# Attention values with the stationary side swapped to two column halves, softmax ahead of convolution taps, and GpSimd's taps in a sum of their own

## The chip, the cores and the metric
The kernel is one program on one core of a Trainium2 chip. The metric is the device time of one execution in microseconds (us); lower is better. A core has TensorE (PE, matmuls; PEld is its weight load), VectorE (DVE), ScalarE (ACT), GpSimd (POOL) and SyncE (SP, which here issues most transfers). They run side by side and wait for each other by semaphores. Matmul results land in PSUM, which holds eight banks of 512 f32 per partition; everything else is in SBUF.

## The reference
256 positions of 1024 channels go through two stacks of two layers each.

```
# stack 1, per layer: rmsnorm -> w_in (14 groups of 256 columns) -> four branches -> w_out, added to x
y_a = conformer_conv(a_u, a_v, ...) * silu(a_z)      # 31-tap depthwise convolution, layernorm, silu
y_b = short_gated_conv(b_b, b_c, b_x, w) * silu(b_z)
y_c = window_gqa(c_q, c_k, c_v, sink) * silu(c_z)    # 4 heads of 64, rope, softmax with a sink logit
y_d = neighborhood_attn(d_q, d_k, d_v, rpb) * silu(d_z)   # 4 heads of 64, learned bias
x = x + concat(y_a, y_b, y_c, y_d) @ w_out
# stack 2, per layer: swiglu FFN, mixer (forgetting attention, dilated attention, HGRN2 recurrence), swiglu FFN
x = x + 0.5 * swiglu(rmsnorm(x), wg, wu, wd)
x = x + concat(fox_attention, dilated_attention, hgrn2) @ w_out
x = x + 0.5 * swiglu(rmsnorm(x), wg, wu, wd)
```

Each attention is softmax(q k^T + bias) v for 256 queries and 256 keys in 4 heads. For the change only this counts: out[query, h] = sum over keys of p[query, key] * v[key, h] / (sum over keys of p), and in stack 1 the result times the gate silu(z).

## The kernel before
**Slots.** The work is a sequence of weight slots. A slot is 128x2048 f32: one group of 256 columns of w_in, two row blocks of w_out, or a part of an FFN matrix. SP loads it into `w_raw`, ACT rounds it (`round_hi`, line 455, w_hi), DVE subtracts (`split_lo`, line 872, w_lo), and PE multiplies hi*hi, hi*lo and lo*hi (lines 1593 to 1595; 1633 and 1636 in the FFN). Three slots are in flight (RING = 3): the load of slot i waits for the split of slot i-3, and the rounding of slot i+3 waits until PE is done with slot i.

**Order.** All order is written out by hand, each engine has one queue, and the queues meet by semaphores. In a mixer, "step i" is projection i of 14 (`ORDER_1`: a_u, a_v, c_q, c_kv, d_q, d_k, d_v, c_z, d_z, b_c, b_x, b_b, b_z, a_z); then four slots of w_out follow. After projection i PE does small work between the big projections.

**Attention units.** A mixer has four units u of 128 queries and 4 heads (two units for each of two attentions), spread over steps 7 to 13, with step i = 7 + u as the start of unit u:
- step 7+u: PE `scores` (line 1733; each head's 64 channels lie on one half of the partitions), DVE `soft` (bias add and row maximum, lines 947 to 956), ACT `softmax_exp` (line 515)
- step 8+u: PE `turn_probs` (transposes, line 1744), ACT `pt_copy` of the transposed probabilities to pT (line 565), DVE `finish` (1/sum)
- step 9+u: PE `values` (line 1753: pT is stationary, 128x128; v moves, 64 columns; result is queries x channels in `mix`), ACT `normed_output` (line 542: four scaled copies `mix` to `o_tm`)
- step 10+u: PE turns o_tm back to channels x queries in `aux` (lines 1823, 1967, 1997), DVE gates it in stack 1 (`gated_y`, line 1104) and splits it to y_hi and y_lo (lines 879, 880); in stack 2 `plain_y` only splits.

In stack 2 the two units with u even have only 128 keys (`causal_keys`), so half the matmuls and transposes. Each f32 matmul shows as two instructions in the profile, each transpose as one. Within a step PE's order is values, turn_probs, scores, output turn.

**DVE's order in a step of stack 1.** Copy of the projection out of PSUM (line 937), then 2 or 3 convolution taps (`taps`, line 1090) in steps 2 to 9, then `finish` and `soft`, then `split_lo` of slot i+3, then gates; in steps 4 and 5 the rope rotation (`rotate`, lines 982 to 987) comes last, and `gated_y` comes last too.

**Convolution.** 31 taps on two channel halves c. DVE sums taps 0 to 19 of half 0. ACT multiplies the other 42 (`tap_products`, line 532) but one into a ring of 5 buffers `fz`, POOL adds them (`add_product`, line 1496): the 31 taps of half 1 first, then, after waiting for DVE's last tap (`conv_part`), the last 11 of half 0 into DVE's sum. `conv_ready` lets PE turn the result (`conv_to_tm`) in the first w_out slot; layernorm statistics follow on DVE (line 1123), POOL takes the root (line 1454), DVE applies it (line 1143), and PE turns it back (line 1840) in the second w_out slot.

**Norms.** POOL's `norm` makes 1/rms by a power (lines 1453, 1454; for the double norm between the stacks lines 1537, 1538), and PE's `spread_rows` (line 1665) spreads it over columns. At the end of a section DVE (`section_end`) adds to x, splits h and splits the first slots of the next section.

Of the kernel before, what the change touches and what calls it, by code (L numbers as in the profile page):

```python
# [23 lines left out]
NH = 4  # L24
# [26 lines left out]
for _i, _n in enumerate(["hq0", "hq1", "hf0", "hf1", "hi0", "hi1", "hg0", "hg1"]):  # L51
# [11 lines left out]
DVE_TAPS = 20  # L63
# [14 lines left out]
                  if kind in ("left", "right") or (kind == "turn" and i in (7, 8)) or (kind == "out" and i >= 10)]  # L78
               + ["cross", "ho0", "out13", "ho1", "hn0", "hn1"])
# [73 lines left out]
def stacks_kernel(nc, a, out):  # L153

    with ExitStack() as ctx:
# [22 lines left out]
        o_tm = sb("o_tm", [P, 2, NH * HD])  # L178
# [258 lines left out]
        def _(act):  # L437
# [96 lines left out]
            def normed_output(un, u, turned):  # L534

                c = 4 * (u % 2)
                act.wait_ge(inv_ready, un + u + 1)
                act.wait_ge(mix_written, un + u + 2)
                if u >= 2:
                    act.wait_ge(aux_written, turned)  # L540
                for s_, h in enumerate(HORDER):
                    ins = nc.scalar.activation(o_tm[:, u % 2, h * HD:(h + 1) * HD], mix[:, h * HD:(h + 1) * HD], ACT.Copy,
                                               scale=row_inv[:, c + s_:c + s_ + 1])
                ins.then_inc(mix_read, 1)
# [82 lines left out]
            for l in range(DEPTH):  # L627
                base, base3, un = l * LAYER_1, l * (LAYER_1 // RING), l * 4
                gates = 0
                for i, name in enumerate(ORDER_1):  # L630
# [9 lines left out]
                    if SC_1 + 2 <= i < SC_1 + 6:  # L640
                        normed_output(un, i - SC_1 - 2, l * AUX_1 + i - SC_1)
# [66 lines left out]
            for l in range(DEPTH):  # L708
# [87 lines left out]
                for i, name in enumerate(ORDER_2):  # L796
# [28 lines left out]
                    if SC_2 + 2 <= i < SC_2 + 6:  # L825
                        u = i - SC_2 - 2
                        normed_output(un, u, ax + AUX_IX_2[f"out{i - 1}"] + 1 if u >= 2 else 0)
# [25 lines left out]
        def _(dve):  # L853
# [56 lines left out]
            def section_end(section, base, slots, factor, split):  # L910
# [13 lines left out]
                split_h(n, (2, 3))  # L924
                split_lo(base + slots, 2)
# [40 lines left out]

            def normed_output(un, u):

                c = 4 * (u % 2)
                dve.wait_ge(mix_written, un + u + 2)  # L970
                for s_, h in enumerate(HORDER):
                    ins = v.tensor_scalar(o_tm[:, u % 2, h * HD:(h + 1) * HD], mix[:, h * HD:(h + 1) * HD],
                                          row_inv[:, c + s_:c + s_ + 1], None, ALU.mult)
                ins.then_inc(mix_read, 1)
# [96 lines left out]
            for l in range(DEPTH):  # L1071
# [25 lines left out]
                def gated_y(u, kt):  # L1097
# [4 lines left out]
                    yv = y_f[:, 0:2 * P].rearrange("p (c s) -> p c s", s=P)  # L1102
                    dve.wait_ge(aux_written, n + 1)
                    v.scalar_tensor_tensor(out=yv, in0=aux[:, 0:2 * P].rearrange("p (c s) -> p c s", s=P), scalar=0.5,
                                           in1=g[:, :, cols], op0=ALU.mult, op1=ALU.mult).then_inc(aux_read, 1)
                    dve.wait_ge(aux_read, n + 2)
                    split_y(yv, kt, cols, yc_ready if u < 2 else yd_ready, l * 2 + u % 2 + 1)

                lnx = proj[:, ix["a_v"], :].rearrange("p (t c) -> p t c", t=NT)
                for i, name in enumerate(ORDER_1):  # L1110
                    if i == 0:
                        dve.wait_ge(rb_ready, l + 1)
                    if name != "d_v":
                        copy_out(base, i, name, l * NPROJ + i)
                    if i == 7:
                        step_aux()
                    if i == 13:
                        gated_y(3, 6)

# [19 lines left out]
                    split_lo(base, i + RING)  # L1139
                    if i == 13:  # L1140
# [4 lines left out]
                        ins.then_inc(aux_read, 1)  # L1145
                    if name in ("a_v", "c_z", "d_z", "b_z", "a_z"):
# [14 lines left out]
                    if l == 0 and i == 6:  # L1161
# [10 lines left out]
                    if i == 5:  # L1172
                        rotate(step_aux(), proj[:, ix["c_kv"], 0:S], cst[:, C_COS:C_COS + S],
                               cst[:, C_SIN:C_SIN + S], 1, kc[:, 0, :])
# [875 lines left out]
```

## Time and profile before
| | us |
|---|---|
| median of 3 executions | 1315.42 (1314.92 to 1316.31) |
| the profiled execution | 1318.41 |
| its span, first to last instruction | 1316.5 |
| first stack | up to about 280 |
| FFNs and mixers of the second stack | from there to the end |

The profile is of one execution. Start times are us from the start of the span. "Busy" of PE contains the modelled end of each matmul, so a matmul shows some 270 ns while another starts every 110 ns: what a matmul costs PE is the distance between starts, which the chain of waits gives (the length of a piece divided by its number of instructions). The granted clock is a share of 2.4 GHz: 1.00 is 2.4 GHz and 0.50 is 1.2 GHz.

### The profile page before, as it was taken

The numbers are of one execution on the slowest core, as the hardware profiler recorded it, in microseconds if no ns is written. First come the engines' busy times: TensorE is split into PE (matmuls) and PEld (weight loads), VectorE is DVE, ScalarE is ACT, GpSimd is POOL, SyncE is SP. The second block draws the span as 40 slices with busy tenths as digits, with TensorE's granted clock in tenths as the row PEclk, the third lists the DMA queues.
The fourth block names the chain that finished last, engine by engine and source line by source line (L and its number), as shares of the span: only waits on it lengthen the run. The fifth ranks groups of instructions, "written<-read, shape, count | busy, mean of one in ns | idle before, by whom it ended". The sixth has DMA issues, their size and how long they took to land.

```text
span 1316.5 us, 21360 instructions
## 1 busy us (share of the span) xinstructions
PE 1288.8 (98%) x8100; PEld 1155.2 (88%) x8100; DVE 978.0 (74%) x1172; ACT 699.1 (53%) x957; POOL 276.0 (21%) x261
## 2 busy tenths in 40 slices
PE   7999999999999999999999999999999999999997
PEld 7989998988888899998888888888889998888886
DVE  5787787779777769767877778877776967777776
ACT  5575457564444487645444445444458663644443
POOL 3655165447000023201000007300011410100000
PEclk9999999999999999999999999999999999999999
DMA  9745473357666545335666665766654524666661
GB/s 275 238 129 152 163 218 122 118 161 206 195 188 189 181 133 184 101 97 160 206 188 189 188 187 162 216 188 189 193 157 142 160 97 127 189 202 188 188 192 50
DMA packets 271551, 224.03 MB, mean 170 GB/s; under 512 B 16012, under 2 KB 254358, under 8 KB 271478
## 3 DMA queue, kind: packets, MB, share of 16 engines
q1 hardware_dynamic: 268720, 217.61, 54.8%
q0 software_dynamic: 880, 2.11, 0.9%
q10 hardware_dynamic: 1878, 3.32, 0.7%
q8 instruction: 48, 0.79, 0.2%
q14 instruction: 25, 0.20, 0.0%
HBM read 221.83 MB, written 3.14 MB: 171 GB/s over the span
## 4 chain that ended last, share of the span: by engine, by line
PE 85%; DVE 7%; ACT 3%; DMA 2%; issue 2%; POOL 1%; SPq 0%; DVEq 0%; POOLq 0%; ACTq 0%
PE wide L1633 24%; PE wide L1636 13%; PE big L1593 8%; PE big L1594 8%; PE big L1595 8%; PE wide L1593 5%; PE wide L1594 5%; PE wide L1595 5%; DVE w_lo L872 2%; DMA w_raw<-in_w_in 2%; PE wide L1902 2%; PE wide L1753 2%; PE big L1733 1%; PE big L1744 1%; ACT w_hi L455 1%
## 5 line engine op out<-in xcount | busy, mean ns | idle before, releaser
L872 DVE TENSOR_TENSOR w_lo<-w_raw,w_hi 128x2048 fp32r<-128x2048 f32 x203 | 471.8, 2325 | 103.0 <-ACT w_hi L455 102.3
L455 ACT ACTIVATE w_hi<-w_raw 128x2048 fp32r<-128x2048 f32 x204 | 389.8, 1912 | 195.3 <-PE big L1595 129.2
L1633 PE MATMUL wide<-h_both,w_hi 128*128 128x512 f32 x1408 | 356.7, 393 | 0.0
L1633 PEld LDWEIGHTS wide<-h_both,w_hi 128*128 128x128 f32 x1408 | 254.6, 189 | 48.6 <-DVE h_both L895 2.0
L1593 PE MATMUL wide<-h_both,w_hi 128*128 128x256 f32 x720 | 208.8, 290 | 0.0
L1636 PEld LDWEIGHTS wide<-h_both,w_lo 128*128 128x128 f32 x1408 | 194.2, 190 | 15.0
L1594 PE MATMUL wide<-h_both,w_hi 128*128 128x256 f32 x720 | 204.1, 284 | 0.0
L1595 PE MATMUL wide<-h_both,w_lo 128*128 128x256 f32 x720 | 204.0, 283 | 0.0
L1636 PE MATMUL wide<-h_both,w_lo 128*128 128x256 f32 x1408 | 198.8, 282 | 0.0
L1593 PE MATMUL big<-w_hi,y_hi 128*128 128x512 f32 x480 | 189.4, 395 | 0.0
L1594 PE MATMUL big<-w_lo,y_hi 128*128 128x512 f32 x480 | 187.3, 390 | 0.0
L1595 PE MATMUL big<-w_hi,y_lo 128*128 128x512 f32 x480 | 187.0, 390 | 0.0
L678 ACT ACTIVATE work<-wide 128x512 f32<-128x512 f32 x88 | 52.5, 597 | 235.3 <-PE wide L1636 235.3
L1453 POOL TENSOR_SCALAR small<-small 128x1 f32<-128x1 f32 (+1 forms) x22 | 4.8, 216 | 796.4 <-ACT probs L459 733.9
L1593 PEld LDWEIGHTS wide<-h_both,w_hi 128*128 128x128 f32 x720 | 138.6, 193 | 3.5 <-issue 2.6
L1594 PEld LDWEIGHTS wide<-h_both,w_hi 128*128 128x128 f32 x720 | 138.7, 193 | 0.1
L1595 PEld LDWEIGHTS wide<-h_both,w_lo 128*128 128x128 f32 x720 | 138.4, 192 | 0.0
L1207 DVE TENSOR_TENSOR work<-wide,work 128x512 f32<-128x512 f32 x88 | 60.7, 690 | 88.1 <-ACT work L678 88.1
L1595 PEld LDWEIGHTS big<-w_hi,y_lo 128*128 128x128 f32 x480 | 90.1, 188 | 19.3
L1593 PEld LDWEIGHTS big<-w_hi,y_hi 128*128 128x128 f32 x480 | 90.3, 188 | 16.9
L1594 PEld LDWEIGHTS big<-w_lo,y_hi 128*128 128x128 f32 x480 | 90.4, 188 | 16.5
L1496 POOL TENSOR_TENSOR work<-work,fz 128x256 f32<-128x256 f32 x82 | 89.9, 1097 | 53.9 <-ACT fz L532 37.1
(247 smaller groups left out, 1536.2 us busy)
## 6 DMA issues: line engine op xcount, KB each, us to landing
w_raw<-in_w_in SPq DMA_DIRECT2D x112, 512.0 KB, 4.7
w_raw<-in_ffn_w_gate SPq DMA_DIRECT2D x88, 512.0 KB, 4.0
w_raw<-in_ffn_w_up SPq DMA_DIRECT2D x88, 512.0 KB, 5.2
w_raw<-in_ffn_w_down SPq DMA_DIRECT2D x88, 512.0 KB, 4.1
w_raw<-in_w_out SPq DMA_DIRECT2D x32, 512.0 KB, 4.3
work<-rpb_shifted SPq DMA_DIRECT2D x32, 64.0 KB, 4.1
rpb_shifted<-rpb_rows POOLq DMA_DIRECT2D x2, 735.0 KB, 8.2
pT<-in_gains ACTq DMA_DIRECT2D x2, 512.0 KB, 5.3
```

The source lines that it names most:

```text
L455: nc.scalar.activation(w_hi[:, r, :], w_raw[:, r, :], ACT.Copy).then_inc(hi_ready, 1)
L678: nc.scalar.activation(tmp_cross[parity].rearrange("p (c s) -> p c s", s=S), wide[:, 2 * parity:2 * parity + 2, S:2 * S], ACT.Copy).then_i ...
L872: v.tensor_tensor(w_lo[:, r, :], w_raw[:, r, :], w_hi[:, r, :].bitcast(F32), ALU.subtract).then_inc(lo_ready, 1)
L1207: v.tensor_tensor(both, wide[:, 2 * parity:2 * parity + 2, 0:S], tmp_cross[parity].rearrange(view, s=S), ALU.add).then_inc(pj_read[parity], 1)
L1496: g.tensor_tensor(acc, acc, fz[:, n % PROD_RING, :], ALU.add).then_inc(prod_used, 1)
L1593: t_.matmul(o, a_hi, b_hi, start=first, stop=False, skip_group_check=True)
L1594: t_.matmul(o, a_hi, b_lo, start=False, stop=False, skip_group_check=True)
L1595: return t_.matmul(o, a_lo, b_hi, start=False, stop=last, skip_group_check=True)
L1633: t_.matmul(o, hi[:, kt, c], h_both[:, kt].rearrange("p a s -> p (a s)"), start=kt == 0, stop=False, skip_group_check=True)
L1636: ins = t_.matmul(o[:, 0:S], lo[:, kt, c], h_hi[:, kt, :], start=False, stop=kt == KT - 1, skip_group_check=True)
L1753: ins = t_.matmul(mix[:, h * HD:(h + 1) * HD], pT[:, (2 * s_ + kt) * P:(2 * s_ + kt + 1) * P], v_of(h, kt), start=kt == 0, stop=kt == keys ...
L1902: ins = t_.matmul(aux[:, h * P:(h + 1) * P], key[:, h * S + tk * P:h * S + (tk + 1) * P], query[:, h * S + tq * P:h * S + (tq + 1) * P], s ...
```

## The change
- `values`: v (128x64) is stationary, the transposed probabilities move (128 columns). Heads 2c and 2c+1 write partitions 0 to 63 and 64 to 127 of the same 128 columns of `mix`. The result is already channels x queries, so `o_tm`, ACT's `normed_output` and the output turn go.
- The scale 1/sum now is needed along the columns: PE spreads it (`spread_inverse`), again in two column halves, into `aux`. In stack 1 DVE multiplies it with the gate and then with `mix`; in stack 2 ACT copies it to SBUF (`inverse_copy`) and DVE multiplies.
- Outputs come one step earlier (u - 2 instead of u - 3). PE does scores ahead of turn_probs.
- Stack 1, DVE: rotations right after the copy; softmax, then gated_y, then taps, then the split. The split of slot 9 moves from step 6 to behind softmax in step 7. Taps are dealt 3, 3, 2, 2, 3, 0, 2, 2, 2, 1 over steps 2 to 11.
- POOL sums its 11 taps of half 0 into a separate buffer and adds that to DVE's sum at the end, so it no longer waits in the middle.
- Between the stacks DVE waits for both roots before it splits slot 2.
- The copies of the sink logits move from step 6 to step 2.

```diff
-DVE_TAPS = 20
+DVE_TAPS_AT = {2: 3, 3: 3, 4: 2, 5: 2, 6: 3, 8: 2, 9: 2, 10: 2, 11: 1}
+DVE_TAPS = sum(DVE_TAPS_AT.values())
...
-        o_tm = sb("o_tm", [P, 2, NH * HD])
+        inv_rows = sb("inv_rows", [P, 2, 2 * P])
...
-            def normed_output(un, u, turned):
...
+            def inverse_copy(u, written):
+                act.wait_ge(aux_written, written)
+                nc.scalar.activation(inv_rows[:, u % 2, :], aux[:, 0:2 * P], ACT.Copy).then_inc(aux_read, 1)
...
                 split_h(n, (2, 3))
+                if n == DEPTH:
+                    dve.wait_ge(rstd_ready, rms_count(n) * 2 + 2)
                 split_lo(base + slots, 2)
...
                 def gated_y(u, kt):
+                    scaled_gate = tmp[:, 0:2 * P].rearrange("p (c s) -> p c s", s=P)
                     dve.wait_ge(aux_written, n + 1)
-                    v.scalar_tensor_tensor(out=yv, in0=aux[:, 0:2 * P]..., scalar=0.5,
+                    v.scalar_tensor_tensor(out=scaled_gate, in0=aux[:, 0:2 * P]..., scalar=0.5,
                                            in1=g[:, :, cols], op0=ALU.mult, op1=ALU.mult).then_inc(aux_read, 1)
                     dve.wait_ge(aux_read, n + 2)
+                    dve.wait_ge(mix_written, un + u + 2)
+                    v.tensor_tensor(yv, mix[:, 0:2 * P]..., scaled_gate, ALU.mult).then_inc(mix_read, 1)
+                    dve.wait_ge(mix_read, un + u + 2)
                     split_y(yv, kt, cols, ...)
...
+                    if i == 4:
+                        rotate(step_aux(), proj[:, ix["c_q"], :], ...)
+                    if i == 5:
+                        rotate(step_aux(), proj[:, ix["c_kv"], 0:S], ...)
...
-                        gated_y(3, 6)
...
-                    if 2 <= i < 10:
-                        taps((i - 2) * DVE_TAPS // 8, (i - 1) * DVE_TAPS // 8)
-                    if i == 9:
-                        dve.sem_inc(conv_part, 1)
...
-                    split_lo(base, i + RING)
+                    if 0 <= u - 2 < 4:
+                        gated_y(u - 2, 4 if u - 2 < 2 else 6)
+                    if i == 7:
+                        split_lo(base, 6 + RING)
+                    if i in DVE_TAPS_AT:
+                        done = sum(n for at, n in DVE_TAPS_AT.items() if at < i)
+                        taps(done, done + DVE_TAPS_AT[i])
+                        if done + DVE_TAPS_AT[i] == DVE_TAPS:
+                            dve.sem_inc(conv_part, 1)
...
+                    if i != 6:
+                        split_lo(base, i + RING)
...
                 def plain_y(i, kt):
-                    aux_in(f"out{i}")
+                    aux_freed(f"out{i}")
+                    dve.wait_ge(mix_written, un + u + 2)
+                    v.tensor_tensor(yv, mix[:, 0:2 * P]..., inv_rows[:, u % 2, :]..., ALU.mult).then_inc(mix_read, 1)
                     split_y(yv, kt, cols, ...)
...
+                part = inv_rows[:, 0, :]
+                link(g.memset(part, 0.0))
                 for k, (c, j) in enumerate(POOL_TAPS):
-                    if (c, j) == (0, DVE_TAPS):
-                        pool.wait_ge(conv_part, l + 1)
...
-                    add_product(l * PRODS + k - 1, conv_acc[:, c])
-                pool.sem_inc(conv_ready, 1)
+                    add_product(l * PRODS + k - 1, conv_acc[:, c] if c else part)
+                pool.wait_ge(conv_part, l + 1)
+                g.tensor_tensor(conv_acc[:, 0], conv_acc[:, 0], part, ALU.add).then_inc(conv_ready, 1)
...
             def values(n, v_of, keys=S):
-                for s_, h in enumerate(HORDER):
+                for c in range(2):
                     for kt in range(keys // P):
-                        ins = t_.matmul(mix[:, h * HD:(h + 1) * HD], pT[:, (2 * s_ + kt) * P:(2 * s_ + kt + 1) * P],
-                                        v_of(h, kt), ...)
+                        for low in range(2):
+                            at = (2 * HORDER[2 * c + low] + kt) * P
+                            ins = t_.matmul(mix[low * HD:(low + 1) * HD, c * P:(c + 1) * P], v_of(2 * c + low, kt),
+                                            pT[:, at:at + P], ...)
+            def spread_inverse(n, u):
+                pe.wait_ge(inv_ready, n + 1)
+                for c in range(2):
+                    for low in range(2):
+                        at = 4 * (u % 2) + HORDER[2 * c + low]
+                        ins = t_.matmul(aux[low * HD:(low + 1) * HD, c * P:(c + 1) * P],
+                                        row_inv[:, at:at + 1].to_broadcast([P, HD]), ident, start=True, stop=True, ...)
...
-                    if 0 <= u - 1 < 4:
-                        turn_probs(l * 4 + u - 1, u - 1)
                     if 0 <= u < 4:
...
+                    if 0 <= u - 1 < 4:
+                        turn_probs(l * 4 + u - 1, u - 1)
-                    if 0 <= u - 3 < 4:
+                    if 0 <= u - 2 < 4:
                         aux_free()
-                        pe.wait_ge(mix_read, l * 4 + u - 3 + 2)
-                        for c in range(2):
-                            ins = t_.transpose(aux[:, c * P:(c + 1) * P], o_tm[...], ident)
-                        ins.then_inc(aux_written, 1)
+                        spread_inverse(l * 4 + u - 2, u - 2)
```

## Rows read from the trace of the kernel before

**Rows 1.** Page, busy us (share of the span) and instructions of two engines.
```profile
PE 1288.8 (98%) x8100; PEld 1155.2 (88%) x8100; DVE 978.0 (74%) x1172; ACT 699.1 (53%) x957; POOL 276.0 (21%) x261
```

**Rows 2.** Waits of PE: waiting line, what it waited for, us, times, longest.
```profile
PE big L1744 <- ACT small L518: 3.5, 2, 1.8
PE wide L1794 <- DVE tmp L982: 2.5, 1, 2.5
PE wide L1840 <- DVE proj L1143: 1.3, 2, 0.6
PE big L1665 <- POOL small L1538: 1.1, 1, 1.1
PE wide L1902 <- DVEq L1278: 0.6, 2, 0.3
```

**Rows 3.** Windows, stretch: us, busy (instructions) by engine, PEclk, DMA share, GB/s.
```profile
55.04:58.45 3.41, 3.41 (x16) 3.23 (x16) 3.30 (x6) 1.72 (x4) 3.17 (x4) 0.50 0.95 284
58.45:61.86 3.41, 3.41 (x30) 3.41 (x30) 3.38 (x2) 0.16 (x1) 3.25 (x3) 1.00 0.46 108
208.64:212.05 3.41, 3.41 (x16) 2.26 (x15) 2.72 (x8) 3.30 (x5) 0.00 (x0) 0.50 0.62 186
```

**Rows 4.** Timeline of DVE, layer 0, steps 4 and 5: start, us, what.
```profile
50.05 1.35 DVE L1090 SCALAR_TENSOR_TENSOR work<-work,parA_all 128x256 f32<-128x256 f32 x2
51.43 2.71 DVE L872 TENSOR_TENSOR w_lo<-w_raw,w_hi 128x2048 fp32r<-128x2048 f32 x1
54.07 0.68 DVE L982 TENSOR_TENSOR tmp<-wide,cst 128x512 f32<-128x512 f32 x1
```

**Rows 5.** Timeline of DVE, layer 0, step 7.
```profile
69.69 2.42 DVE L1090 SCALAR_TENSOR_TENSOR work<-work,parA_all 128x256 f32<-128x256 f32 x3
72.14 1.22 DVE L947 SCALAR_TENSOR_TENSOR probs<-big,cst 128x1024 f32<-128x1024 f32 x1
75.35 2.84 DVE L872 TENSOR_TENSOR w_lo<-w_raw,w_hi 128x2048 fp32r<-128x2048 f32 x1
```

**Rows 6.** Timeline of POOL, layer 0, the first 17 products.
```profile
41.48 22.86 POOL L1496 TENSOR_TENSOR work<-work,fz 128x256 f32<-128x256 f32 x17 [8.55 <-ACT fz L532]
```

**Rows 7.** Timeline of DVE, layer 0, step 13.
```profile
123.75 0.41 DVE L1104 SCALAR_TENSOR_TENSOR y_f<-wide,proj 128x256 f32<-128x256 f32 x1
125.52 0.43 DVE L1123 BATCH_NORM_STATS2 bn_raw<-wide 128x6 f32<-128x256 f32 x1
```

**Rows 8.** Timeline of DVE and POOL between the stacks.
```profile
285.66 2.28 DVE L872 TENSOR_TENSOR w_lo<-w_raw,w_hi 128x2048 fp32r<-128x2048 f32 x1
285.74 2.62 POOL L1538 TENSOR_TENSOR small<-small,minus_half 128x1 f32<-128x1 f32 x1
288.70 0.55 POOL L1538 TENSOR_TENSOR small<-small,minus_half 128x1 f32<-128x1 f32 x1
```

**Rows 9.** Chain of waits, layer 0, steps 8 and 9: start, us, what.
```profile
89.96 1.06 PE big L1733 x8
91.02 0.32 PE wide L1593
91.34 0.11 PE wide L1594
96.95 1.73 PE wide L1753 x16
```

**Rows 10.** Chain of waits, second stack, step 7 (L1733 here has 128 columns).
```profile
521.90 0.67 PE wide L1902 x6
522.58 0.65 PE big L1733 x8
```

**Rows 11.** Groups with shapes: line engine op, tiles, shapes xcount | busy us, mean ns | idle before.
```profile
L1753 PE MATMUL wide<-proj,pT 128*128 128x64 f32 x224 | 26.8, 271 | 0.0
L542 ACT ACTIVATE o_tm<-wide,small 128x64 f32<-128x64 f32 x64 | 14.7, 315 | 0.5 <-issue 0.4
L1104 DVE SCALAR_TENSOR_TENSOR y_f<-wide,proj 128x256 f32<-128x256 f32 x8 | 3.3, 417 | 0.1
```

More of the change, by code:

```diff
@@ L77 @@
                + [f"{kind}{i}" for i in range(6, 13) for kind in ("left", "right", "turn", "out")
-                  if kind in ("left", "right") or (kind == "turn" and i in (7, 8)) or (kind == "out" and i >= 10)]
-               + ["cross", "ho0", "out13", "ho1", "hn0", "hn1"])
+                  if kind in ("left", "right") or (kind == "turn" and i in (7, 8)) or (kind == "out" and i >= 9)]
+               + ["cross", "ho0", "ho1", "hn0", "hn1"])
 AUX_2 = len(AUX_ORDER_2)
@@ L825, in _ @@
                     if SC_2 + 2 <= i < SC_2 + 6:
-                        u = i - SC_2 - 2
-                        normed_output(un, u, ax + AUX_IX_2[f"out{i - 1}"] + 1 if u >= 2 else 0)
+                        inverse_copy(i - SC_2 - 2, ax + AUX_IX_2[f"out{i}"] + 1)
                     if SC_2 + 1 <= i < SC_2 + 5:
@@ L1160, in _ @@
                         bounds_shift()
-                    if l == 0 and i == 6:
+                    if l == 0 and i == 2:
+                        dve.wait_ge(table_in, TABLES)
                         for k in range(DEPTH):
@@ L1165, in _ @@
                                               ).then_inc(sink_ready, 1)
+                    if l == 0 and i == 6:
                         dve.wait_ge(const_in, CONSTS)
                         dve.wait_ge(sink_ready, DEPTH * NH)
-                    if i == 4:
-                        dve.wait_ge(table_in, TABLES)
-                        rotate(step_aux(), proj[:, ix["c_q"], :], cst[:, C_COS:C_COS + S], cst[:, C_SIN:C_SIN + S],
-                               2, proj[:, ix["c_q"], :])
-                    if i == 5:
-                        rotate(step_aux(), proj[:, ix["c_kv"], 0:S], cst[:, C_COS:C_COS + S],
-                               cst[:, C_SIN:C_SIN + S], 1, kc[:, 0, :])
-                    if 0 <= u - 3 < 3:
-                        gated_y(u - 3, 4 if u - 3 < 2 else 6)
                 dve.wait_ge(short_conv, l + 1)
@@ L1385, in _ @@
                         rotate(ax2 + AUX_IX_2[f"turn{i}"], q, cos2[:], sin2[:], 2, q)
-                    if 0 <= u - 3 < 3:
-                        plain_y(i, 0 if u - 3 < 2 else 2)
+                    if 0 <= u - 2 < 4:
+                        plain_y(i, 0 if u - 2 < 2 else 2)
                     if name == "hg0":
@@ L1414, in _ @@
                 head_sums(0)
-                plain_y(NPROJ - 1, 2)
                 output_gate(3, NPROJ - 1)
@@ L1954, in _ @@
                                    causal_keys(u))
+                    if 0 <= u - 1 < 4:
+                        turn_probs(l * 4 + 8 + u - 1, u - 1, causal_keys(u - 1))
                     if i in (7, 8):
@@ L1962, in _ @@
                         ins.then_inc(aux_written, 1)
-                    if 0 <= u - 3 < 3:
+                    if 0 <= u - 2 < 4:
                         aux_free(f"out{i}")
-                        pe.wait_ge(mix_read, l * 4 + 8 + u - 3 + 2)
-                        for c in range(2):
-                            ins = t_.transpose(aux[:, c * P:(c + 1) * P], o_tm[:, (u - 3) % 2, c * P:(c + 1) * P], ident)
-                        ins.then_inc(aux_written, 1)
+                        spread_inverse(l * 4 + 8 + u - 2, u - 2)
                 def hgrn_out(t):
@@ L1990, in w_out @@
                     tm_sum(mb, NPROJ + j, j == 0, j == NWOUT - 1, 2 * grp, between)
-                def last_turn():
-                    aux_free(f"out{NPROJ - 1}")
-                    pe.wait_ge(mix_read, l * 4 + 8 + 3 + 2)
-                    for c in range(2):
-                        ins = t_.transpose(aux[:, c * P:(c + 1) * P], o_tm[:, 1, c * P:(c + 1) * P], ident)
-                    ins.then_inc(aux_written, 1)
                 def turn_out(t):
@@ L2008, in _ @@
                 hgrn_out(0)
-                w_out(0, {1: last_turn, 3: lambda: hgrn_out(1)})
+                w_out(0, {3: lambda: hgrn_out(1)})
                 w_out(1, {1: lambda: turn_out(0), 3: lambda: turn_out(1)})
```

48 lines of the change are left out of this document (20 added, 28 removed).

## The prediction, made before the changed kernel was run

> **What bounds the kernel now.** I read the page first: PE is busy 98% of the span, DVE 74%, ACT 53%, POOL 21% [rows 1]. So time can come from two places only: fewer or shorter matmuls, and PE's own waits with what they do to its clock. The view of waits, for PE alone, gives the second: beside the start-up it waits 3.5 us in two waits of the probability transposes for ACT's exponential, 2.5 us once for DVE's rope product, 1.3 us in two waits for the layernorm result, 1.1 us for POOL's root between the stacks, and 0.6 us in two waits of DVE's queue in stack 2 [rows 2]. The windows show what follows: three stretches of 3.41 us, after the rope wait and after each of the two exponential waits (the middle one, at 78.94, is like its neighbours), have a granted clock of 0.50, that is 1.2 GHz, and hold 16 matmuls where the next 3.41 us at 1.00 hold 30 [rows 3]. No wait of PE under 1.7 us is followed by such a stretch. Matmul prices come from the chain of waits.
>
> **Part 1: DVE's order in stack 1.** The rope wait: in step 4 of layer 0 DVE did two taps (1.35) and a split (2.71) ahead of the rotation's first product at 54.07, whose end PE awaited [rows 4]. The rotation now follows the copy and starts at about 50.1, 4.0 us earlier. PE waited 2.5. All of it goes. What moves back is the split of slot 7, by the rotation's 2.3 us to about 56.4; PE needs it after projection 6, at about 58.4.
>
> The exponential waits: in step 7 three taps (2.42) stand ahead of the softmax, which starts at 72.14 [rows 5], and PE waits 1.7 and 1.8 us in the two layers. Now the softmax starts when the scores are there, some 2.4 us sooner; scores go ahead of the transposes, which makes the transposes due 1.1 us later (a scores piece lasts 1.06) [rows 9]. 3.5 us against 1.8 at most: both waits go. Behind the softmax stand two splits of 2.3 each (slots 9 and 10). I laid DVE's queue out step by step for layer 0: split 9 ends at 71.8 and PE wants it at 74.2; split 10 ends at 74.1 and is wanted at 84; the load of slot 12, which waits for split 9, is issued at 72 and rounded at 80. The taps and the gates behind them end by 83, and the copy of projection 9, ready at 80, is late by 3 us but wanted only at 90. So DVE runs late by up to 3 us in steps 8 to 10 without PE seeing it, and is level again in step 11. In steps 9 to 12 it has one more product of 128x256 per unit, of 0.42 like the present one [rows 11], 1.7 per mixer, all in the cover of 5.8 us projections. If that cover were gone each would cost itself, 6.7 in all.
>
> So the waits give 2.5 + 3.5 = 6.0. Without a wait of that length there is no half-clock stretch: each held 16 matmuls in 3.41 us, which at the rate of the next stretch (30 in 3.41, 0.114 each) take 1.8 to 1.9, so 1.5 is lost in each, 4.5 in three [rows 3].
>
> One new wait speaks against this in layer 0. POOL is behind there: its first 17 products last from 41.48 to 64.34, 1.34 each [rows 6]. ACT's step 6 products wait for POOL's ring of five, and behind them in ACT's queue stand the copy of the second key, for which the first scores wait, and in step 7 the first exponential. PE now comes to the scores at 64.3 instead of 68.7; ACT gets its fifth product off at about 64.8 and the copy done at 65.2. I take +0.9 (bounds: 0 if POOL runs at its 1.1 average, +2.5 if the exponential is late too). Below the length of wait that a half clock followed.
>
> **Part 2: POOL's taps.** POOL no longer stops in the middle for DVE's last tap, but waits at the end; DVE's last tap now comes in step 11, at about 104 in layer 0. The final addition, the table transfers of 4.5 us and the short convolution's product follow on POOL's queue, until about 111, when ACT wants them. PE turns the convolution only in the first w_out slot, at about 116. Hidden. With gated_y(3) moved out of step 13, the layernorm statistics no longer wait for its 1.77 us (123.75 to 125.52) [rows 7] but only for PE's transposes, about 0.5 us earlier; PE's wait of 0.64 shrinks by that in both layers: -1.0.
>
> **Part 3: the wait between the stacks.** POOL's power took 2.62 while DVE's split of slot 2 ran from 285.66, and 0.55 once it was over [rows 8]. With DVE holding the split back, both powers are done at about 287.1, PE comes at 288.2 and its 1.1 us goes. The split ends at 289.4; slot 2 is wanted at 292. -1.1. In stack 2 the output turn of step 10 stood behind DVE's plain_y; now ACT frees the bank, and DVE's two queue waits (0.6) go: -0.6. ACT's exponentials of the recurrence come 2 us later in a step, but DVE wants them one step later.
>
> **Part 4: PE's own work.** Before, values are 224 instructions, in the chain 16 in 1.73, so 0.108 each: 24.2 us [rows 9, 11]. They are bound by loading 128 columns, not by the 64 that move. After, there are as many, with 64 stationary and 128 moving columns, in two column halves. How they go no row shows. The nearest is the scores, where heads lie in two row halves: 8 instructions with 256 columns take 1.06, with 128 columns 0.65 [rows 9, 10]. The difference, 0.41, is 4 times 0.103, the passage of 128 more columns for four pairs, not for eight single ones; and a single full-size instruction of 128 columns takes 0.112 (6 in 0.67) [rows 10]. So the two halves run at the same time, and a pair of N = 128 costs about 0.11. I take that for column halves: 112 pairs, 12.3 us, -11.9. Bounds: no overlap, 0.112 each, 25.1, +0.9; overlap and nothing else, -12.5.
>
> `spread_inverse` adds 16 times 8 instructions, 64 pairs of 0.11, 7.0; the 32 transposes that go cost 0.11 each, 3.5. Net +3.5 (without overlap, +10.8).
>
> Changing between full array and halves is not free: the fixed part of the scores is 0.65 - 4 x 0.103 = 0.24, and the first projection matmul behind them takes 0.32 where the next takes 0.11 [rows 9, 10]. So about 0.2 per change, both ways. Before, a mixer of stack 1 has 8 changes (scores in steps 7 to 10). After, steps 9 and 10 go full, columns, rows, full, columns, full (5), step 11 has 4, step 12 has 2: 20. That is 12 more, in stack 2 as well, 48 in four mixers: 9.6 us. In 28 of them the load that stands exposed has half the columns, half of 0.108 less: -1.5. I take +8.1 (bounds: 0, if a change to column halves costs nothing, and 9.6). On this the Trainium skill has a rule, TensorEngine Tiling (Array Packing), Key Properties: changing the tiling mode drains the engine. The 0.2 above agrees for row halves; no row shows it for columns. PE part: -11.9 + 3.5 + 8.1 = -0.3. The swap of the operands is worth nothing by itself; it pays by mode changes for what it saves.
>
> ACT loses 64 copies of 0.23 (14.7 in all) [rows 11] and gets 8 of 0.5; it is off the path.
>
> **The sum.** -6.0 - 4.5 + 0.9 - 1.0 - 1.1 - 0.6 - 0.3 = -12.6. The profiled execution took 1318.4, so 1305.8 on its terms. It lies 3.0 above the median of the three runs shown, 1315.42, so the forecast for the median is 1302.8.
>
> **The rivals.**
> (a) The stall moves. The first exponential, behind ACT's products and POOL's ring, is late again and the clock falls once or twice more. For: POOL's rate in rows 6, and DVE without reserve in steps 7 to 9. Against: by my layout the transposes are due 0.4 us after the exponential. It gives back one or two waits of 1.7 with their 1.5: 1306 to 1309.
> (b) Mode changes cost less than in rows 9 and 10 where one side is a column half: up to -8.1, so 1294.7. For: a row change does not have to be like a column change. Against: the row pieces show it in both directions.
> (c) Column halves do not overlap. Then values keep 25.1 (+12.8 against the forecast), `spread_inverse` costs 14.3 instead of 7.0 (+7.3), and the mode changes stay: 1302.8 + 20.1 = 1322.9, slower than before. The place is all 16 units. The change is slower once more than 13 of these 20 us come true, at two thirds of the overlap lost. For it: both halves read all 128 partitions of the moving side, which row halves don't. Against: nothing in a row.
> (d) The load of a pair is not hidden behind the pair before it. Half of 0.108 for each of 176 pairs, +9.5: 1312.3. In the rows of values, loads run under the matmul before: 0.108 per instruction is the one load, with the 64 moving columns beside it [rows 9, 11]. The Trainium skill says, in TensorE: Matmul & The Clock Gate, Part 3 (Packing small matmuls, The mechanism), that a weight load overlaps matmuls in flight only when they use other rows of the array; two column halves use the same rows. By that rule this rival holds, and the trace of full-size values speaks against the rule.
>
> **How the numbers follow.** Forecast 0.57, (a) 0.14, (b) 0.11, (c) 0.09, (d) 0.09. The predicted time is 1302.8. The forecast's own spread is some 4 us either way (the switch price of 48 changes at 0.03, and the waits). The range takes in (a), (b) and the lower half of (d), and leaves out (c): 1294.5 to 1312. What can be told from no change is 0.2%, 2.6 us. Slower by that needs (c), or (d) with (a): 0.10. Within it, the upper end of (d) or a partial (c): 0.05. Faster: 0.85.
>
> **What would show it.** PE waits for L1744 and L1794 gone from the view of waits, and windows at 1.00 all through stack 1 (else part 1 is wrong). The chain piece of values at about 0.9 + 0.2 for 16 instructions; 1.8 to 2.0 would be (c), 1.3 to 1.5 (d). The first instruction behind a column piece at 0.3 (if 0.1, (b)). A wait of PE's scores for ACT's second key, near 1 us, in layer 0 only. The FFN stretches of stack 2 keep their length. If stack 1 gains under 9 us or the mixers of stack 2 change by more than 3 us each, my sum was wrong even where the total agrees.

## The result, and the profile after

| | before | after |
|---|---|---|
| median of 4 executions, us | 1315.36 (1314.92 to 1316.31) | 1306.22 (1305.99 to 1307.26) |
| profiled execution, its span | 1318.41, 1316.5 | 1306.36, 1304.5 |
| mean granted clock | 0.994 | 0.999 |

The ratio is 0.9931 (95% interval 0.9914 to 0.9948): the changed kernel is 9.1 us faster. The forecast was 1302.8, which is 3.4 us below what came. By the spans of their profiled executions the two kernels lie 12.0 us apart, where the sum had 12.6.

The page after, for [rows 1]. PE and its loads do 6 and 12 us less, with 96 instructions more:
```profile
PE 1282.4 (98%) x8196; PEld 1143.1 (88%) x8196; DVE 989.9 (76%) x1188; ACT 688.4 (53%) x901; POOL 277.1 (21%) x265
```
The waits of PE, for [rows 2] (line, what it waited for, us, times, longest):
```profile
PE big L1740 <- ACT small L519: 2.5, 2, 1.9
PE wide L1907 <- DVE work L1282: 2.4, 4, 0.6
PE wide L1751 <- DVE y_f L1093: 0.4, 2, 0.2
PE wide L1845 <- DVE proj L1140: 0.4, 1, 0.4
PE big L1589 <- DVE y_lo L871: 0.3, 1, 0.3
```
The rope wait, the wait between the stacks and DVE's queue waits are gone. The transposes of the probabilities (L1740, before L1744) still wait for an exponential, but for another: in both layers it is now that of the second unit, 1.9 and 0.6 us. The windows, for [rows 3], and the stretch at the new wait:
```profile
55.04:58.45 3.41, 3.41 (x31) 1.00 0.26 54
208.64:212.05 3.41, 2.80 (x32) 1.00 0.00 0
79.00:82.41 3.41, 2.44 (x28) 1.00 0.72 251
```
The clock stays at 1.00 (2.4 GHz), even around the wait of 1.9.

The reason for the new wait shows in DVE's timeline in steps 7 and 8 of layer 0 (start, us, what; for [rows 5]; some lines left out):
```profile
66.73 1.21 DVE L940 SCALAR_TENSOR_TENSOR probs<-big,cst 128x1024 f32<-128x1024 f32 x1
...
69.72 5.58 DVE L863 TENSOR_TENSOR w_lo<-w_raw,w_hi 128x2048 fp32r<-128x2048 f32 x2
75.23 1.22 DVE L1155 SCALAR_TENSOR_TENSOR proj<-tanh,proj 128x512 f32<-128x512 f32 x1
76.48 0.69 DVE L930 TENSOR_TENSOR proj<-wide,row_scale 128x512 f32<-128x512 f32 x1
...
77.67 1.23 DVE L940 SCALAR_TENSOR_TENSOR probs<-big,cst 128x1024 f32<-128x1024 f32 x1 [0.22 <-DVE small L957]
```
The first softmax comes 5.4 us earlier than before. Behind it stand two splits, 5.58 us with POOL adding beside them (the sum had 2 x 2.3), and a gate; the second softmax starts at 77.67, its exponential at 81.08, and lasts to 83.2.

PE's own pieces are as long as forecast. The first fence is the chain of waits of before, second stack, step 10, the next that of after:
```profile
553.25 1.73 PE wide L1753 x16
554.99 0.45 PE big L1744 x4
555.43 1.09 PE big L1733 x8
```
```profile
542.19 1.02 PE wide L1751 x16
543.22 1.06 PE big L1729 x8
544.28 0.59 PE big L1740 x4
544.87 0.59 PE wide L1760 x8
545.46 0.32 PE wide L1589
```
Sixteen matmuls of values, eight pairs, take 1.02 instead of 1.73. The transposes cost 0.14 more behind a row piece, and `spread_inverse` costs 0.59.

Where the 12.0 us came from, stage by stage. Each number is a difference of the two profiled executions in the distance between the last matmuls of successive slots:

| stage | forecast | came |
|---|---|---|
| rope wait with its half clock | -4.0 | -4.3 |
| first exponential, two layers, with half clock | -6.5 | -7.2 |
| wait for the second key | +0.9 | 0 |
| wait for the second exponential (step 9) | 0 | +2.6 |
| PE's part in the other steps of stack 1 | -0.3 in all | -0.8 |
| layernorm | -1.0 | -1.2 |
| end of layer 0 (w_out waits for `y_lo`) | 0 | +0.8 |
| between the stacks | -1.1 | -1.4 |
| mixers of stack 2, both | -0.6 | -0.4 |
| start | 0 | -0.1 |
| sum | -12.6 | -12.0 |

Parts 1 to 3 were not run one by one. What each is worth is read from the stage in which it acts. In the row of the first exponential, DVE's earlier softmax and PE's scores ahead of the transposes are not told apart.

### The profile page after: what moved, and what is told of

It is laid out like the page before. It is cut to its first block, busy times and chain, and to the rows that moved or that the text cites. A ratio compares the mean times of both kernels' runs of the same rounds, so it can differ in the third digit from the quotient of the medians.

```text
span 1304.5 us, 21499 instructions
## 1 busy us (share of the span) xinstructions
PE 1282.4 (98%) x8196; PEld 1143.1 (88%) x8196; DVE 989.9 (76%) x1188; ACT 688.4 (53%) x901; POOL 277.1 (21%) x265
## 4 chain that ended last, share of the span: by engine, by line
PE 81%; DVE 11%; issue 2%; ACT 2%; DMA 2%; POOL 1%; SPq 0%; DVEq 0%; POOLq 0%; ACTq 0%
PE wide L1629 25%; PE wide L1632 13%; PE big L1589 8%; PE big L1590 8%; PE big L1591 8%; PE wide L1589 4%; DVE w_lo L863 4%; PE wide L1590 4%; PE wide L1591 4%; DMA w_raw<-in_w_in 2%; PE wide L1907 2%; DVE work L1074 1%; PE big L1653 1%; ACT w_hi L456 1%; PE wide L1751 1%
## 5 line engine op out<-in xcount | busy, mean ns | idle before, releaser
L1491 POOL TENSOR_TENSOR work<-work,fz 128x256 f32<-128x256 f32 x60 | 69.2, 1154 | 28.8 <-ACT fz L533 24.9
```

The source lines that it names most:

```text
L1491: g.tensor_tensor(acc, acc, fz[:, n % PROD_RING, :], ALU.add).then_inc(prod_used, 1)
```

## The experiments

Every run was compared with the kernel before on its own chip, whose median lay between 1315.4 and 1316.2; distances to before are the safer figure.

Spans of single executions need a caution. The last matmul of projection 4 in layer 0 starts between 44.6 and 46.0 us (split9_in_6 and split10_in_8), though these two kernels and after (45.2) do the same up to there. Spans "past the start", below, are counted from this matmul to the last projection matmul.

**The kernel before again**, without an edit.

> The kernel before, unchanged, against itself. The profiled execution of before took 1318.41 us, 3.0 above the median of its plain runs; that of after took 1306.36, 0.1 above its own. Theory: nothing is added by profiling; the executions of before differ among themselves in how many of their long PE waits are followed by a stretch of half clock (1.5 us each). Then executions lie between 1314.9 and 1318.5, the longer ones with the lower mean clock, and a profiled one near 1315 shows one or two stretches of 0.50 instead of three. Rival: a profiled execution of before always has its three stretches and takes 1318, and the plain ones differ by something else. Ratio 1.000 by both.

1316.21 us; over the 55 executions of before in the experiments 1313.5 to 1319.1, the shortest with a mean clock of 0.998, the longest with 0.994. The longer ones have the lower clock: on average 1314.6 at a mean clock of 0.998 (7 executions), 1315.5 at 0.997 (23), 1316.4 at 0.996 (21), 1317.7 at 0.995 (2) and 1318.5 at 0.994 (2). Two of the waits of PE in the profile of before_again, and two windows (at the first exponential of layer 0 and of layer 1):
```profile
PE big L1744 <- ACT small L518: 4.6, 2, 2.8
PE wide L1794 <- DVE tmp L982: 1.4, 1, 1.4
```
```profile
75.23:82.06 6.83, 6.14 (x26) 0.50 0.47 154
207.00:210.41 3.41, 2.69 (x21) 1.00 0.25 67
```
The same kernel has here two half-clock stretches' worth instead of three [rows 3]: none after a rope wait of 1.4, a double one at a wait of 2.8, none at the wait of 1.8 in layer 1 that had one before. And the stall moves even without an edit: against the profile of before, step 5 is 2.7 us shorter, step 8 is 2.3 longer, and step 8 of layer 1 is 1.6 shorter. The execution that I had profiled was long by one stretch too many, so most of the 3.0 above the median lay inside the terms that I then removed. The theory holds.

**Parts 1 to 3 alone.** `values`, ACT's scaled copies and the output turns as before, the rest as after (POOL's partial sum in another free buffer).

> Parts 1 to 3 without part 4: DVE's order in stack 1, POOL's taps summed apart, scores ahead of the transposes, the wait between the stacks; values, their scaled copies on ACT and the output transposes stay as before. Theory: this is the whole gain. Rope wait -4.4 and first exponential wait -3.5 per layer less 2 and 0.7 of the new wait for the second exponential, between the stacks -1.4: the profiled execution comes to 1307 to 1309, the median 7 to 9 us under before, ratio 0.993 to 0.995. Rival: the column halves carry a good part of the gain (their matmuls save 11.9 us of PE's time, and only 3.5 + 8.1 of it was argued to be given back); then this kernel stands 3 us or more above after, 1309.5 or more by the median.

1304.95 us, ratio 0.9917 (0.9903 to 0.9930), span 1303.1. This is the whole gain and more: 11.1 us under before, where I had expected 7 to 9 and where after is 9.1 under. Past the start it is 1.1 us shorter than after. Its one wait for an exponential:
```profile
PE big L1753 <- ACT small L519: 1.4, 1, 1.4
```
The exponential of the second unit comes as late as in after, but PE comes later, since its full-size values take 0.7 us longer (1.73 against 1.02): what the column halves save in step 9 turned into waiting, 2.5 us in after's two layers against 1.4 here. In stack 2, where nothing waits for it, after's part 4 costs 0.3 us per mixer against this kernel. The layernorm wait is gone here too, in both layers, though `gated_y(3)` stands where it stood; see below.

**Part 4 alone**, in before's order of DVE and of PE's pieces.

> Part 4 alone: values stationary in two column halves, spread_inverse, the gates on mix and on the spread inverse; DVE's order, the taps, POOL and the order of PE's pieces (transposes ahead of scores) stay as before. Theory: PE's own work comes out even (by the terms of the prediction -11.9 + 3.5 + 8.1), so this kernel is within 2 us of before: 1313.5 to 1316.5, its stack 2 mixers changed by under 0.5 us each, the rope wait and the waits for the exponentials still there. Rival: the column halves gain by themselves, 1311 or less.

1313.78 us, 2.2 under before, ratio 0.9985 (0.9976 to 0.9994). By span it is 1.4 under before_again, past the start 1.9. Of this 0.2 per mixer is in stack 2, as the theory has it. In each layer of stack 1 0.4 is in the second w_out slot, by `gated_y(3)`, and 0.5 in step 12 and the first w_out slot, where turns of outputs are gone. The rope wait is 0.2 longer, which is within what before varies by.

**The halves apart.**
```
-                for c in range(2):
-                    for kt in range(keys // P):
-                        for low in range(2):
+                for low in range(2):
+                    for c in range(2):
+                        for kt in range(keys // P):
```


> After, with the matmuls of values in another order: all of the lower column half first, then all of the upper one, so that neighbours no longer lie in different halves (the border between the two excepted). Theory: a pair costs one passage only because its two halves run at the same time; apart, 16 instructions take 16 x 0.11 instead of 8 x 0.11 of a piece, so a full piece of values goes from 1.1 to about 1.9 us and the sum over 224 instructions is +10 to +12 us: 1316 to 1318. Rival: the price of an instruction in a column half is its small load, whatever stands beside it; then the order costs nothing and the time stays at 1306.

1310.27 us, 4.1 over after (3.4 by the distances to before): neither the theory's 10 to 12 nor the rival's nothing. The piece of values in step 10 of the second stack, by the chain of waits, where after has 1.02:
```profile
545.01 1.51 PE wide L1751 x16
```
By the starts of single matmuls in such a piece the lower half's start every 0.109, with the fifth of them the first of the upper half starts, 0.006 behind it; for eight instructions both halves go on side by side, and the last four run alone at 0.109. So full pieces grow by 0.5, and pieces with one key tile, four matmuls a half, not at all (10.57 in step 9 of stack 2, as in after). The overlap is real, and it does not need neighbours: the first of the upper half, ninth in the program's order, starts beside the fifth.

**Which split stands where.** Two edits. In the first, split9_in_6, step 7 has one split and slot 9's is in step 6 again; in the second, split10_in_8, slot 10's goes behind the second softmax:
```
-                    if i == 7:
-                        split_lo(base, 6 + RING)
+                    if i in (7, 8):
+                        split_lo(base, i - 1 + RING)
```


> After, with the split of slot 9 back in step 6 (behind that step's three taps), so that step 7 has one split behind its softmax instead of two. Theory: DVE has no time to spare in steps 6 to 8 of stack 1, so the 2.3 to 2.8 us only move: the second exponential is no longer late (waits of 1.9 and 0.6 us gone), but the copy and softmax of step 7 start 2.4 to 2.8 us later and the first exponential is late again, by about 1.8 us in layer 0; the time stays within 1.5 us of 1306.2, more if a half-clock stretch comes back. Rival: the two splits in one step were the fault; both waits go, 1303.7.

> After, with step 7 splitting only slot 9 and step 8 slots 10 and 11 behind its softmax. Theory: the second unit's softmax waits only for DVE's queue; it starts 2.8 us sooner in layer 0 (two splits took 5.58 beside POOL's additions), the exponential with it, and PE's waits of 1.9 and 0.6 us for it go: -2.5, 1303.7. Slot 10 is wanted at 84 and its split ends at about 81. Rival: the buffer that this split frees now comes too late for the load of slot 13, or the third exponential is late in turn: 1306 or more.

1306.63 and 1306.14 us, ratios 0.9932 (0.9918 to 0.9945) and 0.9929 (0.9916 to 0.9943): no gain from either. PE's waits in the first, then in the second:
```profile
PE big L1737 <- ACT small L519: 2.7, 1, 2.7
```
```profile
PE wide L1751 <- DVE y_f L1093: 1.7, 1, 1.7
```
The first brings back the wait for the first exponential, with a half-clock stretch of 6.83 us. The second removes both waits for the second exponential (step 9 of layer 0 falls from 11.57 to 9.64) and gets a wait of values for the gate one step on (9.93 to 11.43): my theory had only the first half. Both say that DVE has no slack in steps 6 to 10 of layer 0, and there a stall only changes its place. In layer 1 it does go: in the second kernel's profile steps 9 and 10 are 0.9 shorter there than in after, and no wait comes for it. That is less than its executions differ by (1305.05 to 1307.26), so the medians do not show it.

**Fewer mode changes.** `spread_inverse` directly behind `values`:
```
                         values(...)
+                        aux_free()
+                        spread_inverse(l * 4 + u - 2, u - 2)
```


> After, with spread_inverse directly behind values in both stacks (both lie in column halves), ahead of the scores and the transposes. Theory (a change of mode costs about 0.2 us wherever it stands): steps 9 and 10 have three changes instead of five, step 11 two instead of four, so 6 fewer per mixer: -1.2 in each mixer of stack 2, and -1.7 in each of stack 1, where in step 9 the whole piece (0.6 and its 0.2) comes to lie in the wait for the second exponential. Together -5.8: 1300.4. Rival: the price is not in the change but in the first load of each piece, which stays exposed; then only the piece hidden in the wait counts, -1 to -1.5, about 1305. Second rival: the bank is not free yet, a wait for DVE takes the place, 1306 or more.

1306.09 us, no gain; the second rival is right. In front of the step the bank is not free and the gate is not done:
```profile
PE wide L1751 <- DVE y_f L1093: 2.0, 2, 1.0
PE wide L1760 <- DVE at_in L1286: 1.4, 4, 0.4
```
Together with the later splits, and with the tap of step 11 handed to POOL:

> The two edits before this one together (slots 10 and 11 split in step 8; spread_inverse behind values), and the tap of step 11 given to ACT and POOL (19 taps on DVE), so that POOL's last addition no longer waits until 106.8 for it and POOL is done with the short convolution some 6 us earlier in layer 0. Theory: -2.5 for the second exponential, -4.8 for 24 mode changes, -0.7 for the layernorm wait of layer 0 (POOL's root there comes 2.2 us late behind the short convolution) and -0.6 for the wait on y_lo behind it: -8.6, 1297.6. Rival: what is gained in steps 8 to 10 comes back as DVE's lateness (third exponential, y_f), 1300 to 1302.

1304.57 us (ratio 0.9914, 0.9900 to 0.9927), not 1297.6: the wait for `y_f` reached 2.6 with a half-clock stretch. The layernorm and `y_lo` waits of layer 0 did go. Its five executions lie far apart, 1301.88 to 1306.28.

**DVE's taps in the pause.** In layer 0 DVE stands still for a weight load, from 33.7 to 40.2, and then has no pause over 0.3 us until 109.
```
-DVE_TAPS_AT = {2: 3, 3: 3, 4: 2, 5: 2, 6: 3, 8: 2, 9: 2, 10: 2, 11: 1}
+DVE_TAPS_AT = {2: 11, 3: 3, 4: 1, 5: 1, 8: 1, 9: 1, 10: 2}
```


> After, with the same 20 taps on DVE dealt out otherwise: 11 in step 2, 3 in step 3, then 1, 1, 0, 0, 1, 1, 2 in steps 4 to 10, none in 11. In layer 0 DVE, ACT and POOL stand idle for a load of weights from 33.7 to 40.2; from 42 to 110 DVE has no pause. Theory (the stall that moves about is one thing, DVE's lateness over steps 6 to 11 of layer 0): 8 more taps in the pause, at 0.5 each without POOL beside them, take 5 to 7 us out of the full stretch. The waits for the second exponential (1.9 and 0.6) go and none comes behind them, values no longer wait 0.5 for y_f, POOL's last addition comes before 106.8, and with it the layernorm wait of layer 0 (0.7) and the wait on y_lo (0.6) go: -4.5, 1301.7. Rival: what limits is ACT's and POOL's part (copies before the exponential, products of 1.1 to 1.6 each) and the waits stay: 1305 or more. Against theory in layer 1: 11 taps need 5.5 us of a shorter pause (3.8), so a split is late there by up to 2 us, seen by nobody.

PE's pieces in the order scores, values, `spread_inverse`, transposes, in both stacks:
```
+                    scores(...)
                     values(...)
-                    scores(...)
-                    turn_probs(...)
                     spread_inverse(...)
+                    turn_probs(...)
```

> After, with PE's pieces of a step in the order scores, values, spread_inverse, transposes, in both stacks: three changes of mode where after has five (four becomes two where there are no scores), and the bank for spread_inverse is asked for one scores piece (0.65 to 1.06) later than with spread_inverse right behind values in front, where PE waited 0.4 for it. Theory (0.2 per change): -0.8 in each mixer of stack 2, its third saving kept by the wait; in stack 1 about -1.5 per layer, part of it inside the wait for the second exponential: -4.6, 1301.6. Rival: a change costs what it costs only at the first load of a piece and the number of changes decides nothing: stack 2 unchanged, 1305 or more.

Both edits together:

> The two edits before this one together. Theory: the savings on PE are no longer swallowed by a wait for DVE: -4.5 for the taps and -1.2 per mixer of stack 1, -0.8 per mixer of stack 2: 1297.7. Rival: the savings of PE make DVE late again and it stops at about 1300.

| | us | ratio | span |
|---|---|---|---|
| taps_early | 1303.64 | 0.9902 (0.9884 to 0.9920) | 1301.8 |
| scores_first | 1303.82 | 0.9902 (0.9886 to 0.9919) | 1302.3 |
| early_and_first | 1299.56 | 0.9872 (0.9855 to 0.9888) | 1297.6 |

The theories were right in kind and too large by 2 us each. DVE's timeline in taps_early, the taps in the pause, 0.52 each where beside POOL they take 0.9:
```profile
33.10 5.17 DVE L1074 SCALAR_TENSOR_TENSOR work<-work,parA_all 128x256 f32<-128x256 f32 x10
40.10 2.29 DVE L863 TENSOR_TENSOR w_lo<-w_raw,w_hi 128x2048 fp32r<-128x2048 f32 x1 [1.82 <-ACT w_hi L456]
...
76.90 1.23 DVE L940 SCALAR_TENSOR_TENSOR probs<-big,cst 128x1024 f32<-128x1024 f32 x1 [0.22 <-DVE small L957]
```
DVE is no longer late at 65 (it waits 3.6 us for the next projection), but the two splits behind the first softmax still put the second at 76.90, so 0.6 of PE's wait for its exponential stays in each layer. The waits for `y_f`, `y_lo` and layernorm are gone. A mode change (from the full array to row or column halves, or back) has its price in scores_first: `spread_inverse` behind values (chain, second stack, step 10) takes 0.44, against 0.59 in after, and the step is 0.34 shorter by two changes, 0.17 each:
```profile
540.45 1.06 PE big L1729 x8
541.51 1.02 PE wide L1751 x16
542.54 0.44 PE wide L1760 x8
542.97 0.59 PE big L1740 x4
```
Alone it is bought with a layernorm wait of 1.5 in layer 0. Together the two edits gain 6.7 us on after, more than the sum of both (5.0), since PE's savings no longer end in a wait; by the distances to before the two figures are 7.5 and 6.7, past the start 6.8 and 5.1. The median is still 1.9 above the 1297.7 of the theory and near the 1300 of its rival (DVE late again). The rival's reason is not what came, for the waits below are short. The shortfall is that of the taps, 2.6 where 4.5 was expected; what scores first adds to them is 4.1, as expected (4.0). early_and_first is the fastest kernel of the study; its waits of PE beside those at the start and in the recurrence:
```profile
PE wide L1760 <- DVE at_in L1286: 0.7, 2, 0.4
PE big L1740 <- ACT small L519: 0.5, 2, 0.3
```

**The worth of part 4 without waits.** order_alone with the taps of taps_early.

> Parts 1 to 3 without part 4, as in order_alone (values full size, their scaled copies on ACT), with the taps dealt out as in taps_early (11 in step 2 of stack 1, none in steps 6, 7 and 11). What is measured is the worth of part 4 once DVE is not late. Theory: this takes the 1.4 us wait for the second exponential of layer 0 and the 0.8 us of the waits on y_lo in w_out: span 1300.7, median about 1302.5, under the 1303.6 of taps_early (part 4 in after's order of pieces costs 0.3 per mixer) and above the 1299.6 of early_and_first (with three changes of mode instead of five part 4 gains). Rival: the column halves pay nothing in any order; then this kernel reaches 1299.6 to 1300.5.

1303.18 us, span 1300.8. The span is the theory's 1300.7, but 1.2 us of what parts it from taps_early (1301.8) lie in the first 45 us. Past the start the two are within 0.2 us, and so are their distances to before (12.8 and 12.6). So in after's order of pieces part 4 is worth nothing that can be told from noise: by the stages it saves 0.8 in stack 1 and costs 0.6 in stack 2. Part 4 and scores first together gain 3.8 past the start, 3.9 by the distances to before (early_and_first). How much of that scores first would give to full-size values is open: that kernel was not run.

## Why the prediction was right, and where it was not

*What bounds the kernel.* That the gain lies in PE's waits and the clock behind them is shown: parts 1 to 3 alone, which leave PE's work as it was, give the whole of it.

*The rope wait and the first exponential.* Right in mechanism and size, -11.5 against -10.5 on the profiled execution. Against before_again the same two rows of the table would read -9.6.

*"DVE runs late by up to 3 us in steps 8 to 10 without PE seeing it."* This step failed. It looked only at what is late behind each split and at when slots are wanted, and it priced both splits at 2.3, where beside POOL they take 2.8. The one thing in steps 7 to 9 that PE awaits, the second softmax, stands behind them. PE saw 2.6 us of it. That the cause is DVE's place in the queue is shown by split10_in_8 and taps_early: the wait went or shrank when the second softmax came sooner. Rival (a) had the mechanism, a stall that moves, but the wrong unit: ACT's and POOL's ring delayed nothing, and no half clock came with it.

*The wait for the second key (+0.9)* did not come: step 7 is 7.01 long in both kernels. ACT did that copy at 62.90, before PE wanted it.

*The layernorm wait.* The size came (-1.2 for -1.0), but the step I named is one of two that each shorten the wait, and I had overlooked the larger one. Before, DVE did the split of slot 16 ahead of applying the layernorm, and the first operation of POOL's root, beside that split, took 2.04. With the split behind, as in order_alone, it takes 0.18 (timelines of POOL, before, then order_alone):
```profile
127.26 2.04 POOL L1453 TENSOR_SCALAR small<-ln_rstd 128x2 f32<-128x2 f32 x1 [2.38 <-DVE ln_rstd L1125]
```
```profile
121.69 0.18 POOL L1461 TENSOR_SCALAR small<-ln_rstd 128x2 f32<-128x2 f32 x1 [0.23 <-DVE ln_rstd L1134]
```
It is the effect of [rows 8], at a place where I did not look for it, and the diff moves that split too. Alone, this is worth 0.8 per layer (order_alone, where `gated_y(3)` stands as before), and `gated_y(3)` alone 0.4 (columns_alone, where that operation still takes 2.04). In layer 0 of after only 0.3 is left of both, for there PE waits for POOL's short convolution.

*Part 2, "hidden".* Not quite. DVE's tap in step 11 holds POOL's last addition until 106.78, and the end of layer 0 is 0.8 late with it; with no tap there (taps_early, all_three) this goes.
```profile
106.78 2.80 POOL L1506 TENSOR_TENSOR work<-work,inv_rows 128x256 f32<-128x256 f32 x1 [7.68 <-DVEq L1136]
```

*Between the stacks* right: POOL's second power now takes 0.55, and PE's wait is gone, -1.4.

*Part 4.* The terms held: a pair at 0.109, `spread_inverse` 0.59 with its change, and 0.17 per change where I had 0.2. Rivals (c) and (d) are refuted by the piece of values, 1.02 for sixteen where (c) needs 1.8 and (d) 1.3. Rival (b) is refuted by the 0.32 of the first projection matmul behind a column piece and by the 0.17. The rule of the Trainium skill that a load overlaps matmuls in flight only in other rows (TensorE: Matmul & The Clock Gate, Part 3) is against this trace, since by it the loads of the pairs would show and the piece would last 1.3; the one on mode changes (TensorEngine Tiling (Array Packing), Key Properties) agrees with it, now for columns too. The forecast of nearly zero for part 4 came out, past the start, as -1.9 on before's order and +1.1 on after's. There 1.1 of its saving ran into the new wait. With the taps early it is -0.2.

*"It lies 3.0 above the median, so the forecast for the median is 1302.8."* This is what made the forecast 3.4 too low. The sum itself was right to 0.6 on the execution it was made for. But the 3.0 were no cost of profiling: most of them were a third half-clock stretch and a longer stall, both among the terms removed. Taken off once, the forecast is 1305.8, against 1306.22. With the rows of before_again in its place (waits of 6.0, two stretches, 3.0) the sum is 11.1 and the forecast 1305.1.

That the sum came so near is in part luck. It lacked 3.4 us of stalls (2.6 in step 9, 0.8 at the end of layer 0). Against them stand the 0.9 of a wait that did not come and some 2 us by which other rows gained more than their terms.

## What to carry to other kernels

A sum made on one execution holds for that execution: before subtracting its distance to the median, ask which of its rows make it long, and count a term that varies (here the half clock) at its average. When an engine has no pause over several steps, reordering it moves the stall and does not remove it (four kernels here within 0.6 us of each other with the wait in different places); look for the pause of the same engine, however early, and move work there first. A saving on the bounding engine counts only where no wait follows it in the same step.

## What the runs showed of the hardware

Whether the clock falls around a wait of PE is not settled by the wait's length alone. Past the start-up, five waits of 2.5 us and more (before 2.5, before_again 2.8, columns_alone 2.8, split9_in_6 2.7, all_three 2.6) each had a stretch at 0.50; waits up to 1.6 had none; of seven from 1.7 to 1.9 two had one (both in before) and five had none (before_again, columns_alone, after, split10_in_8, scores_first). The same wait of 1.8 in the same kernel went both ways. A stretch at 2.7 and 2.8 was 6.83 long, twice the others. What decides between them stays open.

Two column halves of the array work side by side. In pairs, a half's matmul starts 0.006 to 0.007 behind its partner's and the next pair 0.109 later (after). They do so even when their instructions come in blocks: the upper half's first matmul started beside the lower half's fifth (halves_apart).

GpSimd and VectorE slow each other both ways. POOL's operation on 128x2 elements took 2.04 beside a split (before) and 0.18 without (order_alone). DVE's split took 2.8 beside POOL's additions (after) and 2.29 alone, a tap 0.9 and 0.52 (taps_early).
